# Routing work of each pass issued inside the next mixer pass, with the residual kept in DRAM and no barrier between the two halves of the kernel

## The reference, cut to what matters

```python
mod = silu(c) @ w_ada + b_ada                  # 6 vectors per sequence: sh1 sc1 gt1 sh2 sc2 gt2
h = rmsnorm(x, norm1_g) * (1 + sc1) + sh1
b_a, c_a, h_a, v_b, g_b, mg_a, mg_b = split(h @ w_in)          # 1024 -> 4608
y_a = (b_a * dwconv3(c_a * h_a)) @ w_out_a
y_b = silu(layernorm(dwconv31(v_b * sigmoid(g_b)))) @ w_out_b  # both convolutions are causal
x = x + gt1 * ((sigmoid(mg_a) * y_a + sigmoid(mg_b) * y_b) @ w_o)
h2 = rmsnorm(x, norm2_g) * (1 + sc2) + sh2
g = argmax(h2 @ w_group); (e1, e2), w = softmax_top2((h2 @ w_expert)[group g]) * p_g
x = x + gt2 * sum_k w_k * (silu(h2 @ w1[e_k]) * (h2 @ w3[e_k])) @ w2[e_k]   # 16 experts, hidden 256
return rmsnorm(x, final_norm_g), and the last inputs of both convolutions as new states
```

## Time and profile before

| | before |
|---|---|
| median of the runs | 1298.83 us |
| the profiled execution's own time | 1294.24 us |
| its span on the slowest core (core 6) | 1292.6 us |
| the other seven cores' spans | 1271.1 to 1279.3 us |
| TensorE busy with matmuls | 869.2 us, 67% of the span |
| VectorE, ScalarE, GpSimd busy | 523.9, 444.3, 223.4 us |
| mixer passes (with the start) | 0 to 697 us |
| routing | 697 to 911.8 us |
| experts | 911.8 to 1171 us |
| combine | 1171 to 1292.6 us |

### The profile page before, as it was taken

The page is one execution under the profiler, slowest core; times in us unless marked ns, Lnnn a source line. Parts: engine busy times, 40 slices in busy tenths (PEclk is TensorE's granted clock), DMA queues, the critical chain, the costliest instruction groups (busy, mean ns, idle before and its releaser), DMA issues.

```text
span 1292.6 us, 17944 instructions; the slowest of 8 cores (1271.1 to 1292.6 us)
## 1 busy us (share of the span) xinstructions
PE 869.2 (67%) x5272; PEld 457.9 (35%) x5278; DVE 523.9 (41%) x1534; ACT 444.3 (34%) x728; POOL 223.4 (17%) x308
## 2 busy tenths in 40 slices
PE   0367898998899898779875344343488787882322
PEld 0233444544444444345643111121244343432321
DVE  1110446163517352656525334425244333341344
ACT  1313454365336513450662423532122221220121
POOL 1223213101120111012013110220121111004410
PEclk9999999999999999999987666566699998995675
DMA  9999949849882547068233910110499999934534
GB/s 173 170 209 215 228 142 193 250 169 318 303 160 66 192 163 131 2 231 163 87 124 55 174 64 24 66 65 9 112 182 223 223 199 210 202 89 133 154 129 150
DMA packets 135348, 198.86 MB, mean 154 GB/s; under 512 B 6992, under 2 KB 96976, under 8 KB 131920
## 3 DMA queue, kind: packets, MB, share of 16 engines
q0 software_dynamic: 111616, 136.86, 51.1%
q1 hardware_dynamic: 23632, 60.79, 15.0%
HBM read 189.69 MB, written 59.31 MB: 193 GB/s over the span
## 4 chain that ended last, share of the span: by engine, by line
PE 42%; DMA 20%; issue 13%; DVE 12%; ACT 10%; another core or an unknown queue 1%; POOL 1%; DVEq 1%; SPq 0%; ACTq 0%; POOLq 0%
PE ps_all L495 12%; DMA ring<-w_in 7%; DMA wC<-w 7%; PE ps_all L634 7%; PE ps_all L718 5%; PE ps_all L942 3%; PE ps_all L1113 2%; PE ps_all L1115 2%; PE ps_all L1128 2%; DMA vbuf<-sb 2%; DVE yrow L1136 2%; PE ps_all L702 1%; ACT L686 1%; DMA yT<-x3T 1%
## 5 line engine op out<-in xcount | busy, mean ns | idle before, releaser
L495 PE MATMUL ps_all<-hT,ring 128*128 128x448 bf16 (+1 forms) x1440 | 278.4, 353 | 55.0 <-DMA ring<-w_in 23.1
L495 PEld LDWEIGHTS ps_all<-hT,ring 128*128 128x128 bf16 x1440 | 141.4, 100 | 188.9 <-issue 80.4
L634 PE MATMUL ps_all<-ub,dgb 128*128 128x448 bf16 (+1 forms) x620 | 119.6, 338 | 15.4 <-DVE dgb L584 9.8
L356 POOL DMA_DIRECT2D ring<-wcache x104 | 55.1, 530 | 264.0 <-PE ps_all L495 141.3
L584 DVE TENSOR_SCALAR dgb<-identB,vecs_sb 128x128 bf16<-128x128 bf16 x515 | 97.1, 253 | 8.4 <-PE ps_all L634 5.8
L1128 PE MATMUL ps_all<-wC,aT 128*104 128x512 bf16 x256 | 72.5, 384 | 25.5 <-DVE yrow L1136 17.3
L634 PEld LDWEIGHTS ps_all<-ub,dgb 128*128 128x128 bf16 x620 | 60.4, 97 | 68.0 <-issue 25.5
L1177 PE MATMUL ps_all<-dgw,gat 128*128 128x128 bf16 (+1 forms) x272 | 26.9, 274 | 71.7 <-DVE x3T L1180 42.4
L1133 ACT ACTIVATE yrow<-ps_all 104x512 bf16<-104x512 f32 x64 | 38.2, 597 | 99.4 <-PE ps_all L1128 99.4
L942 PE MATMUL ps_all<-h2f,wr_sb 128*20 128x512 f32 (+2 forms) x80 | 39.3, 662 | 46.7 <-DVE h2T L933 27.8
L1136 DVE CAST yrow<-ps_all 104x512 bf16<-104x512 f32 x64 | 44.3, 692 | 51.3 <-PE ps_all L1128 42.4
(11 more groups left out here) (177 smaller groups left out, 1277.7 us busy)
## 6 DMA issues: line engine op xcount, KB each, us to landing
ring<-wcache POOLq DMA_DIRECT2D x104, 512.0 KB, 5.1
wcache<-ring POOLq DMA_DIRECT2D x26, 512.0 KB, 10.2
xslots<-dga SPq DMA_DIRECT2D x4, 3328.0 KB, 16.9
xsb<-xslots SPq DMA_DIRECT2D x16, 832.0 KB
yslots<-yrow SPq DMA_DIRECT2D x16, 832.0 KB
ring<-w_ada POOLq DMA_DIRECT2D x24, 512.0 KB, 10.6
ring<-w_in POOLq DMA_DIRECT2D x18, 512.0 KB, 13.8
wA<-w POOLq DMA_DIRECT2D x16, 512.0 KB, 17.8
```

The lines of the kernel that those rows point to most:

```text
L356: S.add(POOL, lambda e, slot=slot, bid=store_as: [e.dma_start(out=ring[slot][:, :], in_=wc_d[bid])], reads=[("wc", store_as)], writes=[("r ...
L495: return [e.matmul(PS(bank, n), wv[:, kc, j * 128:(j + 1) * 128], hT[:, kc, 0:n], start=(kc == 0), stop=(kc == NDC - 1)) for kc in range(NDC)]
L634: return [e.matmul(outp(sg_, bank), dgb[:, r, :], mv_b(sg_, c, k), start=(k == 0), stop=(k == 30)) for sg_, bank in zip(P.segs, banks)]
```

## The change

The routing work of pass P-1 (`rows_norm2`) is cut into pieces and added inside mixer pass P: the squares and the norm in `in_proj_gates(P)`, the router at the start of `convs(P)`, the choice of experts in `in_proj(P+1)`, ranks before `mixer_out(P)`, slots and the first two tiles' transposes and scatters before `in_proj_ba(P+1)`, the other two before `out_proj(P)`. Pass 4 takes that of pass 3 in its convolutions and gates. Only the routing of pass 4 itself stands alone. Tiles are now of 112 tokens (19 of them), the unit of combine is the pass. The residual has three buffers of one pass in SBUF; each pass stores it to DRAM (`x2_d`) and combine loads it back. All buffers live in one arena; a buffer that takes over another's bytes waits only for that one (`lend`), and the barrier is gone. The convolution states are loaded by casting DMAs straight into their strided places, and the old part of the returned state is copied from DRAM to DRAM. The blocks 12 to 19 of `w_ada` move into the first `in_proj`. There are 5 weight buffers for the experts, `ex_Y` uses 4 banks, the gates 4 banks, combine 6 banks and 3 buffers of x.

```diff
+        xb = []                                    # residual: 3 buffers of one pass
+        for i in range(3):
+            t_, o_, n_ = raw("xb%d" % i, [128, NDC, PW], F32)
...
-        sb_stage = vbuf[:, 0:4 * NSEQ_S * 30].rearrange("p (c s j) -> p c s j", c=4, s=NSEQ_S)
-        dma(SP, "ld_sb", vbuf[:, 0:4 * NSEQ_S * 30], sb_d[:, :], ...)
+        S.add(POOL, lambda e: [e.dma_start(out=ua_s[:, :, :, 0:2], in_=sa_d.rearrange("p (a b c) -> p a b c", a=4, b=NSEQ_S)),
+                               e.dma_start(out=ub_s[:, :, :, 0:30], in_=sb_d.rearrange("p (a b c) -> p a b c", a=4, b=NSEQ_S)),
+                               e.dma_start(out=triB[:], in_=tri_d[:, :])], ...)
+        S.add(SP, lambda e: [e.dma_start(out=nbs_dv[:, :, 0:26], in_=sb_d.rearrange("p (a c) -> p a c", c=30)[:, :, 4:30])], ...)
...
+        for P in PASSES:
+            n2 = rows_norm2(PASSES[P.idx - 1]) if P.idx else None
+            mods = {0: [8, 9, 10, 11], 2: [20, 21, 22, 23]}.get(P.idx, [])
+            if nxt is not None:
+                n1s = norm1_sq(nxt, 4)
+                if n2 is not None:
+                    fl = [f for a, b in zip(n2["sq"], n1s) for f in (a, b)] + [nop, n2["ss"], nop, nop, nop]
+                    for f in n2["apply"]:
+                        fl += [f, nop]
+                proj_bank["set"] = (0, 1, 6, 7)
+                in_proj_gates(P, filler=fl)
+                proj_bank["set"] = (0, 1)
+                norm1(nxt)
+                ...
+                fl = [(lambda dc=dc: norm1_dc(nxt, dc)) for dc in range(NDC)]
+                if n2 is not None:
+                    fl = [n2["router"]] + fl + [n2["ltr"]]
+                convs(P, filler=fl)
+                for hb in mods:
+                    mod_compute(hb)
+                ln_ops = layernorm_b(P)
+                if P.idx == 0:
+                    late = []
+                    for hb in (16, 17, 18, 19, 12, 13, 14, 15):
+                        late += [lambda hb=hb: mod_block(hb), nop]
+                else:
+                    late = chunked(n2["route"], 18)
+                in_proj(nxt, filler=zipl(ln_ops, late))
+                if n2 is not None:
+                    n2["rank"]()
+                mixer_out(P)
+                if n2 is not None:
+                    run_all(n2["slots"])
+                    run_all(n2["rows"][0:2])
+                in_proj_ba(nxt)
+                if n2 is not None:
+                    run_all(n2["rows"][2:4])
+                    run_all(n2["weights"])
+                out_proj(P)
+            else:
+                gen_diags(P, NDG - 1)
+                sq_, ap_ = n2["sq"], n2["apply"]
+                fl = [lambda: run_all(sq_[0:2]), lambda: run_all(sq_[2:4]), n2["ss"]]
+                fl += [lambda i=i: run_all(ap_[2 * i:2 * i + 2]) for i in range(4)] + [n2["router"], n2["ltr"]]
+                convs(P, filler=fl)
+                ln_ops = layernorm_b(P)
+                fl = zipl(ln_ops, chunked(n2["route"], 14))
+                fl += [n2["rank"]] + chunked(n2["slots"], 4) + n2["rows"]
+                in_proj_gates(P, filler=fl)
+                run_all(n2["weights"])
+                mixer_out(P)
+                out_proj(P)
+            S.add(SP, ... e.dma_start(out=x2_d[:, :, P.t0:P.t0 + P.n], in_=xb[P.idx % 3][:, :, 0:P.n]) ..., name="st_x2")
...
-        S.add(SP, lambda e: [], writes=list(S.last_w.keys()) + ["__bar__"], name="barrier_sp")
-        for eng in (PE, ACT, DVE, POOL):
-            S.add(eng, lambda e: [], reads=["__bar__"], name="fence_" + eng)
...
+        NWS = 5
+        n2 = rows_norm2(PASSES[4])
+        for ex in range(4):
+            load_expert(ex)
+        run_all(n2["sq"]); n2["ss"](); run_all(n2["apply"]); n2["router"](); n2["ltr"]()   # five lines in the file
+        run_all(n2["route"]); n2["rank"](); run_all(n2["slots"]); run_all(n2["rows"]); run_all(n2["weights"])
         flag_op = overflow()
+        load_expert(4)
...
-                    bank = 6 + yb["n"] % 2
+                    bank = (6, 7, 2, 3)[yb["n"] % 4]
...
+            if ex == 2:
+                load_x2(PASSES[0])
+            if ex == 3:
+                load_x2(PASSES[1])
+            if ex == 12:
+                load_x2(PASSES[2])
...
-        gather(ST_[0]); gather(ST_[1]); combine(ST_[0])
-        for i, st in enumerate(ST_): combine(i+1), gather(i+2), final_norm(st)
+        gather(PASSES[0]); gather(PASSES[1]); combine(PASSES[0])
+        for P in PASSES: combine(P+1), gather(P+2), final_norm(P), load_x2(P+3)
```

More of the change, by code:

```diff
@@ L79, in add @@
         for k in writes:
+            for o in self.old.pop(k, ()):
+                self.dead.add(o)
+                if o in self.last_w:
+                    deps.add(self.last_w[o])
+                deps.update(self.readers.get(o, {}).values())
             w = self.last_w.get(k)
@@ L83, in add @@
             deps.update(self.readers.get(k, {}).values())
+        for k in list(reads) + list(writes):
+            assert k not in self.dead, (name, k)
         who = op if op.is_dma else eng
@@ L280, in build_program, with sbA, K1 @@
         S.add(ACT, lambda e: [e.activation(out=scT[:], in_=cT[:], func=AF.Silu)], reads=["cT"], writes=["scT"], name="silu_c")
[L282 to L286, removed]
+        def sbA(name, shape, dt, keys):
+            t_, o_, n_ = raw(name, shape, dt)
+            S.lend(keys, o_, n_)
+            return t_
+        def K1(name, n):
+            return [(name, i) for i in range(n)]
@@ L294, in build_program @@
[L294 to L304, removed]
@@ new lines, in rows_norm2, with nop, run_all, zipl @@
+            out["rows"] = [lambda t_=t_: rows_out(t_) for t_ in P.tiles]
+            return out
+        bound = {}
+        U32 = mybir.dt.uint32
+        def nop():
+            pass
+        def run_all(lst):
+            for f in lst:
+                f()
+        def zipl(a, b):
+            out = []
+            for i in range(max(len(a), len(b))):
+                out.append(lambda i=i: (a[i]() if i < len(a) else None, b[i]() if i < len(b) else None))
+            return out
+        def chunked(lst, k):
+            q = -(-len(lst) // k)
+            return [lambda i=i: run_all(lst[i:i + q]) for i in range(0, len(lst), q)]
@@ new lines, in place @@
+        def place(name, shape, dt, unit=None, off=None):
+            t, off, per = raw(name, shape, dt, off)
+            S.region(name, off, per)
+            if unit is not None:
+                nb = unit * (2 if dt == BF16 else 4)
+                for i in range(per // nb):
+                    S.region((name, i), off + i * nb, nb)
+            return t
+        NWS = 5
+        wslot = [xo[2], xo[0], o_ca, o_ua, o_zsq]
+        wA = [place("wA%d" % i, [128, NDC, DE], BF16, off=wslot[i]) for i in range(NWS)]
@@ L1083, in build_program @@
+        n2 = rows_norm2(PASSES[4])
+        for ex in range(4):
+            load_expert(ex)
+        run_all(n2["sq"])
+        n2["ss"]()
+        run_all(n2["apply"])
+        n2["router"]()
+        n2["ltr"]()
+        run_all(n2["route"])
+        n2["rank"]()
+        run_all(n2["slots"])
+        run_all(n2["rows"])
+        run_all(n2["weights"])
         flag_op = overflow()
+        load_expert(4)
         allxs = [("xs", gt) for gt in range(NTT)]
```

773 lines of the change are left out of this document (385 added, 388 removed).

## The result

The changed kernel takes 1452.53 us (median of 4 runs, 1446.5 to 1463.7) beside 1298.6 us for the kernel before on the same chip: ratio 1.120, 95% interval 1.112 to 1.127. It is slower by 12%; the prediction said 1278 us, and 1195 to 1340 as its range.

What follows compares the result with a forecast made beforehand. Routing and combine were taken as chains between engines, the passes as bound by TensorE, start and experts by DMA. Terms -171 +135 +34 +25 +16 -3 -24 -33 gave -21 us, so 1278 us, range 1195 to 1340.

Steps and rivals of the forecast that it cites:

- Routing: Stage after the passes: only pass 4's routing, 43.2 us, stays of 214.4; gain 171 us, bounds 160 to 175.
- Passes 1 to 3: Mixer passes taking in routing: matmuls, GpSimd queue, ScalarE, expert choice and clock add 45 us each, range 15 to 65.
- The two stalls: Passes 1 to 3: TensorE idles 10 to 15 us before `in_proj_ba` and before `out_proj`, ring loads queued behind scatters.
- The start: Strided state loads and old-state copy, small pieces at 9 or 23 ns, add 25 us; bounds 11 to 93.
- Rival B: Start: strided state loads cost the casting price, 93 us and not 25, total 1346 us; chance 0.15.
- `w_ada` in pass 0: Eight more weight blocks in pass 0: 30 us less 14 of free DMA time, so +16, range 0 to 30.
- The -3 in later passes: Later passes: two sets of `w_ada` blocks fewer, 1.6 us each, save 3 us.
- Pass 4: Matmuls, transposes, VectorE in the convolutions, and 20 us for ring loads behind scatters: +34 us, range 15 to 50.
- Experts: Expert stage: earlier weight loads and no bank waits, less two residual loads: 259 to 235 us, -24; bounds -35 to +10.
- two waits as additive: Expert stage: TensorE's waits for weights, 10.7 us, and for PSUM banks, 17.3 us, both go, together 28.
- Rival C: Experts and combine keep their time because DMA is what they wait for, total 1335 us; chance 0.17.
- Combine: Combine stage: three buffers end the waits for stores, 121 to 88 us, -33; bounds -45 to 0.

Runs made afterwards that it cites:

- e7: Changed kernel with the edits of e2, e3 and e4, and the second state assembled in SBUF and stored once contiguously: 1256.7 us, ratio 0.973.
- e4: Changed kernel with two w_in and four w_o block loads of passes 1 to 3 issued on GpSimd ahead of that pass's scatters: 1347.5 us, ratio 1.048.
- e3: Changed kernel with the four fills of the slot array no longer naming hT as read, place and bytes unchanged: 1397.7 us, ratio 1.083.
- e2: Changed kernel with casting history loads made contiguous on SP's queue plus two VectorE copies, SP's DRAM-to-DRAM copy staying at the start: 1418.1 us, ratio 1.098.
- e1: Changed kernel with SP's DRAM-to-DRAM copy of history columns moved from the start to behind the mixer passes: 1435.1 us, ratio 1.112.
- e5: Changed kernel with eight w_ada blocks moved from pass 0 back to passes 2 to 4, second norm's shift and scale zero until then: 1411.3 us, ratio 1.094.
- e8: e7 with the scatters of pass 3's rows moved, in pass 4, from the gates to behind mixer_out and out_proj's ring loads: 1227.4 us, ratio 0.951.
- e9: e8 with the residual loads of the first three passes issued behind experts 13, 14 and 15: 1217.1 us, ratio 0.940.
- e12: Kernel before with the change's four PSUM banks for the expert outputs and its order of h banks, nothing else: 1286.0 us, ratio 0.994.
- e6: Changed kernel with the three residual loads moved from inside the expert stage to behind its last expert: 1419.4 us, ratio 1.097.

## Why the prediction was wrong, step by step

Against the traces of core 6 the sum said -21 us and +161 was measured; 182 us are missing. By its terms:

- **Routing**, -171 said, -158 measured (214 to 56 us), just short of the bounds (160 to 175). Some 3 us of the miss are the chain itself: from `out_proj` to the issue of the last scatter it takes 46.0 us on the median core. The rest is the landing of that scatter: 11.2 us from its issue to the first load of slots for 1.9 before and 2.0 in e7 (worked out from the traces, median of the eight cores). **The store of the new state columns, 8192 pieces of 16 bytes, had no term**; e7, which stores them contiguously, has a routing of 47 us on core 6, where 43 were said.
- **Passes 1 to 3**, +45 each said. Right for passes 2 and 3: +43 and +46. The two stalls came where they were said, 15.06 and 12.44 us for 16.8 and 12.7, with the scatters ahead of the loads, and e4 gives them back. What is left then in e7, 135 to 137 us for 120 to 121, is the 15 to 16 us that the prediction had for TensorE's extra matmuls, ScalarE, route and clock.
- **Pass 1** took 38 us more than that. No step of the prediction covers it: **it priced the moved steps without the fills**, which the change puts from behind a norm to ahead of one and one pass earlier in the order. e3 shows it.
- **The start**, +25 said, +60 measured (+51 on the chips of the experiments). **The step that failed is the price of a piece of the copy, taken from short packets of SP's queue (23 ns).** The copy of 8192 pieces alone costs 34 us (e2 less e7, 85.5 less 51.3), 67 ns of an engine for each (34.2 x 16 / 8192), three times the 23. The 16384 casting pieces cost 17 us together (e1 less e7), 16 ns each, what was counted for the two kinds on average. (These are prices by the length of the stage, as the prediction counted them; the packets' own records overlap, with shares above 1.) Rival B put 93 us on the start and the blame on the casts; the cost lies between 25 and 93, and most of it is the copy from DRAM to DRAM. First weights some 60 us late was one of the prediction's own signs of being wrong.
- **`w_ada` in pass 0**, +16 said; e5 measures 25 to 29, and all of pass 0 is 38 longer on the median core, 44 on core 6. The full price of 30 was right, **the 14 us of free DMA time taken off it were not to be had**. Why the free share of 144 to 204 us was not used is not shown; that the loads are in order and wait for TensorE to free a buffer is likely. Of the other 9 to 15 us of pass 0, 8 stand in the first `in_proj` (`in0`, 62 to 66 us in all kernels with the change for 56.6), and their cause is open. The -3 in later passes did not come: with the blocks back there, e5 is no longer than the changed kernel (164.4 for 163.7, 220.2 for 220.7).
- **Pass 4**, +34 said, +51 on core 6. Its queue part was 25.5 (e8) and not 20. The convolutions of pass 4 are still some 20 us longer in e9 (192.0 for 156.1, less pass 3's 16). The groups of TensorE in them, in e9:

```profile
L722 PE MATMUL ps_all<-ub,dgb 128*128 128x256 bf16 x124 | 23.0, 295 | 10.4 <-DVE dgb L672 4.4 <-ACT vsq L737 4.2 <-ACT dgb L669 1.3
...
L871 PE MATMUL ps_all<-h2f,wr_sb 128*20 128x448 f32 x16 | 7.5, 630 | 0.0
```

  The router takes 7.5, which was in the prediction's 8.4. TensorE idles 10.4 for diagonals and evictions, which share VectorE and ScalarE with the second norm, for 1.9 in the kernel before; the prediction had 4 for that. No run isolates it.
- **Experts**, -24 said, +11 measured. **The step that failed took two waits as additive that cover each other**: e12 turns the one into the other at no gain. Rival C was right for this stage, and a stage that stays at 259 us (here 270) was another of the prediction's own signs. The stage waits for its weight loads, and the residual adds 18 us to them (e6), where two loads of some 2 us were counted. Its first load of slots takes 15.64 us for 6.60, 9 of the 11; in e7, with no store of small pieces beside it, 9.83. TensorE's waits in the changed kernel's stage, core 6; the 35.4 is the wait for the first load of slots, 16.8 in the kernel before:

```profile
PE ps_all L1180 <- DMA xsb<-xslots: 53.6, 4, 35.4
PE ps_all L1191 <- DMA wC<-w: 19.3, 8, 6.6
```

- **Combine**, -33 said, -19 measured. The waits for stores went, but the buffer of the first block has to be stored and then loaded with the fourth before the next step can begin, which the prediction named only as "5 MB more". VectorE in the changed kernel's combine:

```profile
1407.36 4.86 DVE L1300 SCALAR_TENSOR_TENSOR x2b<-x2b,vecs_sb,rbt 128x448 f32<-128x448 f32 x8 [1.86 <-ACT rbt L1298]
1419.22 4.82 DVE L1278 SCALAR_TENSOR_TENSOR x2b<-ps_all,modT,x2b 128x448 f32<-128x448 f32 x8 [7.00 <-DMA x2b<-x2s]
```

Misses of the sum: start 35, `w_ada` and pass 0 28, fills 38, passes 2 and 3 -1, pass 4 17, routing 13, experts 35, combine 14, the -3 of later passes 3: together 182. Of these, three came for the most part from DMA work where DMA was full already (start, `w_ada`, experts), 98 us. The rivals held them one by one, and the range had no case for them together. The fills and the store of small pieces were in no case.

## What to carry to other kernels

When work is moved, lay out every queue that it passes, and put loads that a fast engine will ask for ahead of anything in the same list that waits: here six loads, moved up ahead of the scatters in each of three passes, gave 84 us. Count waits on a bound stage once, by the resource that is last when the others are gone. And keep strided pieces of tens of bytes off the DMA queues: contiguous transfers and copies on engines that had time gave 50 to 60 us at the start and some 15 in the routing.

## What was not expected of the hardware

SP's copy from DRAM to DRAM in 104-byte pieces cost 67 ns of an engine each, the casting loads of 4 and 60 bytes 16 ns. The DMA queues of the changed kernel in its first 60 us (packets, MB, share):

```profile
q1 hardware_dynamic: 9968, 3.05, 81.2%
q0 software_dynamic: 8208, 0.03, 60.8%
```

Only 3.08 MB moved there at a summed share over 1.4. The Trainium skill, "DMA: Bandwidth & Descriptors", section "Measured (HBM→SBUF, 128 partitions, SWDGE, issued from GpSimd)", gives about 10.5 ns per packet for a load of 4 KB, 64 packets in 0.67 us. That is time elapsed; counted so, the copy took 4.2 ns a piece (34.2 us / 8192) and the casting pieces 1.0 ns (16.8 / 16384). The figure of that small load does not price pieces by the thousand here, and the measurement decides.

A DMA issue on GpSimd is not free of the engines' load: its second strided load began 54 us after the first had been issued, 14 us when SP's copy was away, with no semaphore in between. In both runs it began within 0.4 us of the first one's landing (58.5 and 18.3 us), but behind the second, with as many pieces, GpSimd went on at once. The Trainium skill, "Perfetto Trace Analysis", section "DMA Instruction — SWDGE (GPSIMD)", says that more descriptors may be generated than fit into the buffer; by that GpSimd would have to stand until the engines have emptied it. The two runs do not contradict this, and do not show the buffer itself.
